# Banded attention with products of 128 rows by 128 columns, keys in two blocks of 128, and the norm ahead of the next mask

## The chip, the cores and the metric

The kernel runs on one core of a Trainium2 chip. The metric is device time in microseconds (us) from one launch, the median of several runs. The engines are named as in the profile: PE (TensorE, matrix products), PEld (its weight loads), DVE (VectorE), ACT (ScalarE), POOL (GpSimd) and SP (SyncE, which issues DMAs here).

## The reference

One inference step of a one-layer encoder: three mixing branches, a gated merge, and a PEER layer of retrieved experts, for a prompt of 512 frames and a sample of 32 frames of a running stream. The change touches one branch, the sliding-window attention. It has 4 KV heads of 4 query heads each, head size 64. A query in chunk c (64 frames) reads the keys of chunks c-2 to c, so 192 keys; a learned sink takes part in the softmax. From `swa_prompt`, where `band` puts the three chunks beside each other:

```python
    kb, vb = band(k), band(v)
    s = jnp.einsum('bnqgrd,bnkgd->bngrqk', q, kb).astype(jnp.float32) * SWA_HEAD_DIM ** -0.5
    koff = jnp.arange(nk) - SWA_BACK_CHUNKS * CHUNK
    s = s + rel_bias(rel_table, koff[None, :] - jnp.arange(CHUNK)[:, None])
...
    s = jnp.where(valid[None, :, None, None, None, :], s, NEG)
    p = sink_softmax(s, sinks).astype(vb.dtype)
    o = jnp.einsum('bngrqk,bnkgd->bnqgrd', p, vb).reshape(B, S, SWA_HEADS * SWA_HEAD_DIM)
```

The sample's 32 queries (`swa_sample`) read a cache of 128 keys and their own 32.

## The kernel before

The program is a row of stages, each between barriers of all engines. In `stage_swa` the order of the work on each engine is written out by hand; semaphore counts (`Steps`) tie the engines together. Beside the attention PE works off a part of the input projection: `later.share` gives it *slices*. A slice is one block of 128 input features of a projection block and takes six products of 128 rows by 128 columns by 272 (L254, L256, L258, two each). Weights for these arrive as pieces of eight slices: SP loads them (L210), POOL splits each in two float32r parts, L221 and L225. `SWA_SHARES = (3, 3, 2, 3, 3, 2)` says how many slices stand at each position of a head; a piece is used up behind each position with two. When a projection block is complete ACT copies it out of PSUM (L420), and the slices of position 6 and position 0 need that buffer again.

The stage first does four projection blocks and loads the bias rows. Then come four heads `g`, each of nine units `u`: chunks 0 to 7 of the prompt, and unit 8, the sample. In a unit 2 pairs of query heads lie side by side as 128 rows. PE's order in a unit is: scores of u+1 (L1492, stationary the queries, 64 rows by 128 columns), two or three slices, transposes of the probabilities `pn` of u (L1510, one for each block of 64 keys and pair), values of u-1 (L1527, stationary 64 rows by 64 columns of `v_tok`). A float32 product counts as two instructions in the profile, a transpose as one. DVE masks the scores (L1643), puts the sink beside them (L1648), takes the maximum (L1651), and norms: reciprocal (L1658) and product `pn` (L1663). ACT takes the exponentials (L1571), copies the transposed probabilities to `p_t` (L1582) and the result out (L1597). Key count is 64 in chunk 0, 128 in chunk 1, 192 from chunk 2 on, 160 in the sample. In the profile `128*64 128x128` is a stationary side of 128 rows and 64 columns and a moving side of 128 columns.

## Time and profile before

| | us |
|---|---|
| median of 3 runs (lowest, highest) | 5074.0 (5071.29, 5079.49) |
| the profiled execution, its span | 5081.78, 5080.0 |
| PE busy in the span | 4933.8 (97%) |
| DVE, ACT, POOL busy | 3172.1, 1100.0, 2855.1 |
| ahead of the heads of `stage_swa` | 1165 to 1224 |
| the four heads of `stage_swa` | 1224 to 1443 |

Busy PE is time in which at least one product is in flight; products are pipelined, so it does not say at what pace they go. Start times in the timeline do. PEclk in a window is the mean granted clock as a share of 2.4 GHz, whose other level is 1.2 GHz.

### The profile page before, as it was taken

What the parts mean: (1) busy time and instruction counts of PE and PEld (TensorE: products, weight loads), DVE (VectorE), ACT (ScalarE), POOL (GpSimd) and SP (SyncE); (2) the same over time, 40 slices, a digit from 0 to 9 for tenths busy, and PEclk for the clock granted to TensorE, in tenths of its full rate; (3) what the DMA queues carried; (4) which work ended last, traced back from release to release, by engine and by line L of the source; (5) the groups of instructions that cost most, each with busy time, mean ns of one, the idle gap of its engine ahead of it and who ended that gap; (6) DMA issues with size and microseconds to landing.
All of it is one profiled execution on the core that took longest, in us unless ns stands there. A gap on an engine that the chain in (4) does not pass through costs nothing. (4 is left out here: it accounts for less than half of the span.)

```text
span 5080.0 us, 87718 instructions
## 1 busy us (share of the span) xinstructions
PE 4933.8 (97%) x32144; PEld 4804.1 (95%) x32144; DVE 3172.1 (62%) x4701; ACT 1100.0 (22%) x1607; POOL 2855.1 (56%) x1698
## 2 busy tenths in 40 slices
PE   8999999999999998999999999999999999999998
PEld 8999999998888787999999999999999999999998
DVE  5477777772222433413057886888786888888865
ACT  4133333331322433201012111122221000000001
POOL 7400000004223333555567787888887999999986
PEclk9999999999999999999999999999999999999999
DMA  7333333334233445533334337889998888888852
GB/s 266 108 127 126 126 126 126 126 127 121 89 110 145 149 165 191 176 131 120 111 131 140 136 131 283 327 323 326 326 328 302 293 311 303 311 301 313 301 201 105
DMA packets 343019, 1010.57 MB, mean 199 GB/s; under 512 B 39696, under 2 KB 132080, under 8 KB 307200
## 3 DMA queue, kind: packets, MB, share of 16 engines
q1 hardware_dynamic: 165760, 526.23, 30.1%
q0 software_dynamic: 36864, 268.45, 14.0%
q10 hardware_dynamic: 140192, 213.34, 11.9%
q8 instruction: 109, 1.79, 0.1%
q14 instruction: 94, 0.77, 0.0%
HBM read 882.26 MB, written 126.76 MB: 199 GB/s over the span
## 5 line engine op out<-in xcount | busy, mean ns | idle before, releaser
L221 POOL TENSOR_SCALAR w_hi<-w_raw 128x1024 fp32r<-128x1024 f32 x702 | 778.7, 1109 | 1983.0 <-PE ps L753 940.1
L225 POOL TENSOR_TENSOR w_lo<-w_raw,w_hi 128x1024 fp32r<-128x1024 f32 x702 | 1734.2, 2470 | 131.8 <-POOL w_hi L221 128.1
L254 PE MATMUL ps<-h_hi,w_hi 128*128 128x416 f32 (+1 forms) x3936 | 1137.1, 328 | 25.5 <-POOL w_lo L225 7.2
L258 PE MATMUL ps<-h_hi,w_lo 128*128 128x416 f32 (+1 forms) x3936 | 1118.5, 323 | 0.0
L256 PE MATMUL ps<-h_lo,w_hi 128*128 128x416 f32 (+1 forms) x3936 | 1111.3, 322 | 0.0
L254 PEld LDWEIGHTS ps<-h_hi,w_hi 128*128 128x128 f32 x3936 | 687.9, 190 | 44.5 <-issue 40.0
L254 PE MATMUL ps<-ex_c_hi,w_hi 128*128 128x416 f32 x2048 | 719.1, 351 | 9.5 <-DVE ex_c_lo L2877 8.6
L258 PE MATMUL ps<-ex_c_hi,w_lo 128*128 128x416 f32 x2048 | 723.9, 353 | 0.0
L256 PE MATMUL ps<-ex_c_lo,w_hi 128*128 128x416 f32 x2048 | 715.9, 350 | 0.0
L256 PEld LDWEIGHTS ps<-h_lo,w_hi 128*128 128x128 f32 x3936 | 687.8, 190 | 6.0
L258 PEld LDWEIGHTS ps<-h_hi,w_lo 128*128 128x128 f32 x3936 | 685.3, 190 | 2.8
L2904 DVE TENSOR_TENSOR ex_y<-ps,ex_y 128x416 f32<-128x416 f32 x512 | 296.9, 585 | 202.4 <-PE ps L258 200.7
L751 PE MATMUL ps<-in_t_hi,w_hi 128*128 128x272 f32 x1408 | 405.4, 288 | 0.9 <-ACT rows_out L866 0.9
L753 PE MATMUL ps<-in_t_hi,w_lo 128*128 128x272 f32 x1408 | 405.7, 288 | 0.0
L752 PE MATMUL ps<-in_t_lo,w_hi 128*128 128x272 f32 x1408 | 405.5, 288 | 0.0
L254 PEld LDWEIGHTS ps<-ex_c_hi,w_hi 128*128 128x128 f32 x2048 | 385.1, 188 | 13.1 <-issue 10.9
L256 PEld LDWEIGHTS ps<-ex_c_lo,w_hi 128*128 128x128 f32 x2048 | 385.7, 188 | 6.4
L258 PEld LDWEIGHTS ps<-ex_c_hi,w_lo 128*128 128x128 f32 x2048 | 384.9, 188 | 2.3
L2291 DVE SCALAR_TENSOR_TENSOR g_sb_u_rows<-g_sb_u_rows,ps 128x2048 f32<-128x2048 f32 x128 | 291.8, 2280 | 139.1 <-DMA g_sb_u_rows<-peer_u,sp_expert 138.9
L730 DVE TENSOR_TENSOR w_lo<-in_sums,w_hi 128x1024 fp32r<-128x1024 f32 x176 | 215.6, 1226 | 206.2 <-ACT w_hi L708 204.1
L2303 DVE SCALAR_TENSOR_TENSOR ps<-ex_v_rows,sp_dot,ps 128x2048 f32<-128x2048 f32 x127 | 297.8, 2345 | 15.5 <-DMA ex_v_rows<-peer_v,sp_expert 15.5
L753 PE MATMUL ps<-h_hi,w_lo 128*128 128x272 f32 x1056 | 304.5, 288 | 0.0
(319 smaller groups left out, 8168.4 us busy)
## 6 DMA issues: line engine op xcount, KB each, us to landing
w_raw<-weights SPq DMA_DIRECT2D x906, 512.0 KB, 3.8
up<-up_out ACTq DMA_DIRECT2D x128, 208.0 KB, 5.7
gate<-g_sb_g ACTq DMA_DIRECT2D x13, 2048.0 KB, 15.0
proj<-rows_out ACTq DMA_DIRECT2D x97, 272.0 KB, 2.0
sp_first<-up ACTq DMA_DIRECT2D x16, 832.0 KB, 7.4
ex_up<-up ACTq DMA_DIRECT2D x16, 832.0 KB, 9.0
ex_gate<-gate ACTq DMA_DIRECT2D x16, 832.0 KB, 17.9
sp_first<-proj ACTq DMA_DIRECT2D x48, 272.0 KB, 3.6
```

Of the source, the lines that this page charges most:

```text
L221: pool.tensor_scalar(self.whi[:, slot, :], self.raw[:, slot, :], 1.0, 1.0, ALU.mult, ALU.mult).then_inc(self.hi_done, 1)
L225: pool.tensor_tensor(self.wlo[:, slot, :], self.raw[:, slot, :], self.whi[:, slot, :].bitcast(F32), ALU.subtract).then_inc(self.split_done, 1)
L254: pe.matmul(acc, hi, x, start=first, stop=False)
L256: pe.matmul(acc, hi, x, start=False, stop=False)
L258: mm = pe.matmul(acc, lo, x, start=False, stop=last)
L730: dve.tensor_tensor(self.core.wlo[:, slot, :], self.source(name), self.core.whi[:, slot, :].bitcast(F32), ALU.subtract).then_inc(self.did_ ...
L751: pe.matmul(out, hi, x_hi(k), start=k == 0, stop=False)
L752: pe.matmul(out, hi, x_lo(k), start=False, stop=False)
L753: mm = pe.matmul(out, lo, x_hi(k), start=False, stop=k == PIECE_K - 1)
L2291: dve.scalar_tensor_tensor(row_of_slot, row_of_slot, 1.0, self.token_rows, ALU.mult, ALU.mult, accum_out=self.dot[:, s:s + 1]).then_inc(se ...
L2303: dve.scalar_tensor_tensor(self.token_rows, buf[:, s % GATHERS, :], c, self.token_rows, ALU.mult, ALU.add).then_inc(self.summed, 1)
L2904: dve.tensor_tensor(y[:, j, 0:TD], ps[:, 4 + j % 4, 0:TD], y[:, j, 0:TD], ALU.add).then_inc(added, 1)
```

## The change

Tiles with 64 rows get 128, the upper half zero (written by DVE at the start of the stage, PE waits for it on `cleared`), so that the scores' products have 128 rows. Keys go in blocks of 128: two transposes a pair in place of three, into 128 rows; `v_tok` holds at each chunk the 128 tokens from its start, so a value product takes 128 rows by 128 columns (the second 64 columns are the next tile's and their results are not read), two blocks in place of three. The last 64 columns of the second block of `pn` are zero for the prompt. On DVE, `normed(u)` stands ahead of `masked(u + 1)`.

```diff
-        q, q_s = two("q", [SWA_HD, N_CHUNKS, SWA_GROUP, CHUNK]), two("q_s", [SWA_HD, SWA_GROUP, DEC_SEQ])
-        k, v = two("k", [SWA_HD, T]), two("v", [SWA_HD, T])
-        cache_k, cache_v = two("cache_k", [SWA_HD, SWA_WINDOW]), two("cache_v", [CHUNK, 2, SWA_HD])
-        v_tok = sb("v_tok", [CHUNK, NB, SWA_HD])
+        q, q_s = two("q", [P, N_CHUNKS, SWA_GROUP, CHUNK]), two("q_s", [P, SWA_GROUP, DEC_SEQ])
+        k, v = two("k", [P, T]), two("v", [SWA_HD, T])
+        cache_k, cache_v = two("cache_k", [P, SWA_WINDOW]), two("cache_v", [SWA_WINDOW, 2, SWA_HD])
+        v_tok = sb("v_tok", [SWA_WINDOW, NB + 1, SWA_HD])
...
-        pn = sb("pn", [P, 2, 2, BAND])
-        p_t = sb("p_t", [CHUNK, 2, 2, 3 * P])
+        pn = sb("pn", [P, 2, 2, 2 * SWA_WINDOW])
+        p_t = sb("p_t", [SWA_WINDOW, 2, 2, 2 * P])
...
-                dve_names += [f"s{u + 1}", f"sink{u + 1}", f"max{u + 1}"]
+                dve_names += [f"inv{u}", f"pn{u}", f"s{u + 1}", f"sink{u + 1}", f"max{u + 1}"]
...
-                return 2 * DEC_SEQ, SWA_WINDOW + DEC_SEQ, [CHUNK, CHUNK, DEC_SEQ]
-            n = min(u, 2) + 1
-            return P, n * CHUNK, [CHUNK] * n
+                return 2 * DEC_SEQ, SWA_WINDOW + DEC_SEQ, [SWA_WINDOW] * 2
+            n_keys = (min(u, 2) + 1) * CHUNK
+            return P, n_keys, [min(n_keys, SWA_WINDOW)] + [SWA_WINDOW] * (n_keys > SWA_WINDOW)
+
+        def span_of(u):
+
+            return (SEQ, DEC_SEQ) if u == N_CHUNKS else (u * CHUNK, min(SWA_WINDOW, SEQ - u * CHUNK))
...
-            sp.dma_start(k[n][:, :], k_rows[g]).then_inc(head_loaded[n], 16)
+            sp.dma_start(k[n][0:SWA_HD, :], k_rows[g]).then_inc(head_loaded[n], 16)
...
-            sp.dma_start(cache_v[n][:, :, :], io["cache_sv"][g].rearrange("(b t) d -> t b d", t=CHUNK)
-                         ).then_inc(head_loaded[n], 16)
+            sp.dma_start(q_s[n][0:SWA_HD, :, :], of_head[:, :, SEQ:T]).then_inc(head_loaded[n], 16)
+            sp.dma_start(cache_k[n][0:SWA_HD, :], io["cache_sk"][g]).then_inc(head_loaded[n], 16)
+            sp.dma_start(cache_v[n][:, 0, :], io["cache_sv"][g]).then_inc(head_loaded[n], 16)
...
             pe.wait_ge(rows_copied, 1)
+            pe.wait_ge(dve_s.sem, dve_s.at("cleared"))
...
-                                          pn[0:n_rows, u % 2, pair, j * CHUNK:j * CHUNK + w],
+                                          pn[0:n_rows, u % 2, pair, j * SWA_WINDOW:j * SWA_WINDOW + w],
...
-                        if u < N_CHUNKS:
-                            values = v_tok[0:w, u + 1 - len(widths) + j, :]
+                        if u == N_CHUNKS and j == 0:
+                            values = cache_v[g % 2]
                         else:
-                            values = cache_v[g % 2][:, j, :] if j < 2 else v_tok[0:w, N_CHUNKS, :]
-                        mm = pe.matmul(ps[0:SWA_HD, 4 + u % 2, pair * n_rows:(pair + 1) * n_rows], values,
+                            tile = max(u - 2, 0) if j == 0 else u
+                            values = v_tok[0:w, tile:tile + 2, :]
+                        mm = pe.matmul(ps[:, 4 + u % 2, pair * n_rows:(pair + 1) * n_rows],
+                                       values.rearrange("t two d -> t (two d)"),
...
-                for b, (t0, w) in enumerate(BLOCKS):
+                for b in units:
+                    t0, w = span_of(b)
...
-                n = len(widths) * n_rows
-                if u < N_CHUNKS:
-                    i = act.activation(p_t[:, u % 2, :, 0:n], ps[0:CHUNK, 2:4, 0:n], ACT.Copy)
-                else:
-                    act.activation(p_t[:, u % 2, :, 0:2 * n_rows],
-                                   ps[0:CHUNK, 2:4, 0:2 * n_rows], ACT.Copy)
-                    i = act.activation(p_t[0:DEC_SEQ, u % 2, :, 2 * n_rows:n],
-                                       ps[0:DEC_SEQ, 2:4, 2 * n_rows:n], ACT.Copy)
+                i = act.activation(p_t[0:w, u % 2, :, 0:n], ps[0:w, 2:4, 0:n], ACT.Copy)
...
+                full = N_CHUNKS - 1
+                act.activation(v_tok[:, 0:full, :],
+                               ps[:, 4, 0:full * SWA_HD].rearrange("t (b d) -> t b d", d=SWA_HD), ACT.Copy)
+                act.activation(v_tok[0:CHUNK, full, :], ps[0:CHUNK, 4, full * SWA_HD:N_CHUNKS * SWA_HD],
+                               ACT.Copy).then_inc(*act_s.did("v0"))
...
+            for n in range(2):
+                for x in (q[n], q_s[n], k[n], cache_k[n]):
+                    dve.memset(x[SWA_HD:P], 0.0)
+                dve.memset(cache_v[n][:, 1, :], 0.0)
+            dve.memset(v_tok[:, N_CHUNKS - 1:NB + 1, :], 0.0)
+            dve.memset(pn[:, :, :, :], 0.0).then_inc(*dve_s.did("cleared"))
...
                 for u in units:
+                    normed(u, g)
                     if u + 1 < NB:
                         masked(u + 1, g)
-                    normed(u, g)
```

The other tiles are sliced `[0:SWA_HD]` where DMAs write them, as `k` is here.

PE, head 0 of the stage, one full chunk (`ps` is PSUM, `x5` stands for five such rows, the last two rows begin the next slices), before:

```order
L1510 MATMUL ps<-const_sb,swa_sb_pn 64x128 [waits swa_dve,swa_act]
L1510 MATMUL ps<-const_sb,swa_sb_pn 64x128 x5
L1527 MATMUL ps<-swa_sb_p_t,swa_sb_v_tok 64x128 [waits swa_act]
L1527 MATMUL ps<-swa_sb_p_t,swa_sb_v_tok 64x128 x5
L1492 MATMUL ps<-swa_sb_k,swa_sb_q 128x192 [waits swa_dve]
L1492 MATMUL ps<-swa_sb_k,swa_sb_q 128x192
L254 MATMUL ps<-h_hi,w_hi 128x272 [waits split_done]
L254 MATMUL ps<-h_hi,w_hi 128x272
```

and in the changed kernel (its L1513, L1531 and L1495 are L1510, L1527 and L1492 of before):

```order
L1513 MATMUL ps<-const_sb,swa_sb_pn 128x128 [waits swa_dve,swa_act]
L1513 MATMUL ps<-const_sb,swa_sb_pn 128x128 x3
L1531 MATMUL ps<-swa_sb_p_t,swa_sb_v_tok 128x128 [waits swa_act]
L1531 MATMUL ps<-swa_sb_p_t,swa_sb_v_tok 128x128 x3
L1495 MATMUL ps<-swa_sb_k,swa_sb_q 128x192 [waits swa_dve]
L1495 MATMUL ps<-swa_sb_k,swa_sb_q 128x192
L254 MATMUL ps<-h_hi,w_hi 128x272 [waits split_done]
L254 MATMUL ps<-h_hi,w_hi 128x272
```

Transposes go from six to four, value products from six to four, all of 128 result rows; the order and the semaphores waited for stay.

DVE, from the start of head 0, before:

```order
L1643 SCALAR_TENSOR_TENSOR swa_sb_s<-ps,swa_sb_bias 128x2x64 [waits swa_bias_loaded,swa_table_loaded,swa_pe]
L1648 COPY swa_sb_s<-swa_sb_sinks 128x2
L1651 TENSOR_REDUCE swa_sb_neg_max<-swa_sb_s 128x2 [waits swa_dve]
L1643 SCALAR_TENSOR_TENSOR swa_sb_s<-ps,swa_sb_bias 128x2x128 [waits swa_pe]
L1648 COPY swa_sb_s<-swa_sb_sinks 128x2
L1651 TENSOR_REDUCE swa_sb_neg_max<-swa_sb_s 128x2 [waits swa_dve]
L1658 RECIPROCAL swa_sb_inv<-swa_sb_total 128x2 [waits swa_act]
L1663 TENSOR_TENSOR swa_sb_pn<-swa_sb_p,swa_sb_inv 128x2x64 [waits swa_dve]
```

and in the changed kernel (L1651, L1656, L1659, L1666, L1671 are L1643, L1648, L1651, L1658, L1663 of before), behind the memsets:

```order
L1651 SCALAR_TENSOR_TENSOR swa_sb_s<-ps,swa_sb_bias 128x2x64 [waits swa_bias_loaded,swa_table_loaded,swa_pe]
L1656 COPY swa_sb_s<-swa_sb_sinks 128x2
L1659 TENSOR_REDUCE swa_sb_neg_max<-swa_sb_s 128x2 [waits swa_dve]
L1666 RECIPROCAL swa_sb_inv<-swa_sb_total 128x2 [waits swa_act]
L1671 TENSOR_TENSOR swa_sb_pn<-swa_sb_p,swa_sb_inv 128x2x64 [waits swa_dve]
L1651 SCALAR_TENSOR_TENSOR swa_sb_s<-ps,swa_sb_bias 128x2x128 [waits swa_pe]
L1656 COPY swa_sb_s<-swa_sb_sinks 128x2
L1659 TENSOR_REDUCE swa_sb_neg_max<-swa_sb_s 128x2 [waits swa_dve]
```

The reciprocal and `pn` of chunk 0 moved from behind the mask and maximum of chunk 1 to ahead of them, and so on through the head.

## Rows read from the trace of the kernel before

**Rows 1.** The page: busy time, share of the span and count of instructions of each engine.

```profile
PE 4933.8 (97%) x32144; PEld 4804.1 (95%) x32144; DVE 3172.1 (62%) x4701; ACT 1100.0 (22%) x1607; POOL 2855.1 (56%) x1698
```

**Rows 2.** Windows ahead of the heads, heads 0, 2, 3: us, busy PE PEld DVE ACT POOL, PEclk.

```profile
1165.00:1224.30 59.30, 54.77 (x405) 53.45 (x403) 0.00 (x0) 2.87 (x5) 24.30 (x15) 0.94 0.70 170
1224.30:1279.00 54.70, 51.16 (x372) 44.45 (x372) 18.57 (x45) 21.22 (x60) 18.12 (x12) 0.97 0.17 54
...
1334.00:1388.50 54.50, 52.13 (x392) 45.47 (x390) 15.64 (x45) 19.94 (x59) 14.85 (x9) 1.00 0.34 107
1388.50:1443.00 54.50, 50.57 (x368) 43.90 (x367) 16.69 (x45) 19.96 (x59) 10.97 (x7) 0.97 0.08 25
```

**Rows 3.** Waits of PE, 1224 to 1443 us: total us, times, longest.

```profile
PE ps L1510 <- DVE swa_sb_pn L1663: 10.0, 14, 2.0
PE ps L1510 <- ACT swa_sb_p L1571: 1.5, 1, 1.5
```

**Rows 4.** Timeline, one chunk of head 3: start us, us, engine, line, operation.

```profile
1405.41 0.42 PE L258 MATMUL ps<-h_hi,w_lo 128*128 128x272 f32 x2
...
1405.66 0.82 PE L1510 MATMUL ps<-const_sb,swa_sb_pn 128*64 128x128 f32 x6
...
1408.52 0.56 DVE L1643 SCALAR_TENSOR_TENSOR swa_sb_s<-ps,swa_sb_bias 128x384 f32<-128x384 f32 x1 [4.11 <-PE ps L1492]
...
1409.77 0.15 DVE L1658 RECIPROCAL swa_sb_inv<-swa_sb_total 128x2 f32<-128x2 f32 x1
1409.99 0.46 ACT L1571 ACTIVATE swa_sb_p<-swa_sb_s,swa_sb_neg_max 128x193 f32<-128x193 f32 x1 [2.00 <-DVE swa_sb_inv L1658]
1410.10 0.56 DVE L1663 TENSOR_TENSOR swa_sb_pn<-swa_sb_p,swa_sb_inv 128x384 f32<-128x384 f32 x1 [0.18 <-DVE swa_sb_inv L1658]
...
1410.79 0.19 ACT L1571 ACTIVATION_READ_ACCUMULATOR swa_sb_p<-swa_sb_s,swa_sb_neg_max 128x1 f32 x1
1410.80 0.81 PE L1510 MATMUL ps<-const_sb,swa_sb_pn 128*64 128x128 f32 x6 [0.76 <-DVE swa_sb_pn L1663]
...
1411.55 1.52 PE L1527 MATMUL ps<-swa_sb_p_t,swa_sb_v_tok 64*64 64x128 f32 x12
...
1411.75 2.34 POOL L225 TENSOR_TENSOR w_lo<-w_raw,w_hi 128x1024 fp32r<-128x1024 f32 x1 [0.18 <-POOL w_hi L221]
...
1413.00 0.91 PE L1492 MATMUL ps<-swa_sb_k,swa_sb_q 64*128 64x192 f32 x4
...
1414.20 0.41 PE L256 MATMUL ps<-h_lo,w_hi 128*128 128x272 f32 x2
...
1416.38 0.82 PE L1510 MATMUL ps<-const_sb,swa_sb_pn 128*64 128x128 f32 x6
```

**Rows 5.** Groups by form on PE, 1223 to 1444 us: count, busy us, mean ns.

```profile
L1527 PE MATMUL ps<-swa_sb_p_t,swa_sb_v_tok 64*64 64x128 f32 x336 | 43.4, 274 | 0.0
L1510 PE MATMUL ps<-const_sb,swa_sb_pn 128*64 128x128 f32 x168 | 23.9, 275 | 11.6 <-DVE swa_sb_pn L1663 10.0 <-ACT swa_sb_p L1571 1.5
```

**Rows 6.** Timeline of PE in the memory stage, products of 128 rows by 128 columns.

```profile
1519.24 1.16 PE L1785 MATMUL ps<-ma_sb_p_t,ma_sb_v_tok 128*128 128x128 f32 x8
1520.15 0.49 PE L254 MATMUL ps<-h_hi,w_hi 128*128 128x272 f32 x2
...
1527.96 1.03 PE L1761 MATMUL ps<-ma_sb_k,ma_sb_q 128*128 128x256 f32 x4
...
1529.08 0.41 PE L256 MATMUL ps<-h_lo,w_hi 128*128 128x272 f32 x2
```

**Rows 7.** Timeline, head 3, chunk 2: VectorE beside GpSimd.

```profile
1395.92 2.40 POOL L225 TENSOR_TENSOR w_lo<-w_raw,w_hi 128x1024 fp32r<-128x1024 f32 x1 [0.18 <-POOL w_hi L221]
...
1396.52 1.82 DVE L1648 COPY swa_sb_s<-swa_sb_sinks 128x2 f32<-128x2 f32 x1
...
1399.83 0.38 PE L1510 MATMUL ps<-const_sb,swa_sb_pn 128*64 128x128 f32 x2 [1.53 <-ACT swa_sb_p L1571]
```

**Rows 8.** Window behind the wait in rows 7; the columns as in rows 2.

```profile
1400.00:1405.00 5.00, 5.00 (x25) 4.20 (x24) 1.81 (x5) 2.12 (x8) 0.00 (x0) 0.66 0.00 0
```

More of the change, by code:

```diff
@@ L1401, in stage_swa @@
                 act_names += [f"e{u + 1}_0", f"e{u + 1}_1"]
-                dve_names += [f"s{u + 1}", f"sink{u + 1}", f"max{u + 1}"]
+                dve_names += [f"inv{u}", f"pn{u}", f"s{u + 1}", f"sink{u + 1}", f"max{u + 1}"]
             pe_names += [f"t{u}"] + ([f"o{u - 1}"] if u else [])
             act_names += [f"t{u}"] + ([f"o{u - 1}"] if u else [])
-            dve_names += [f"inv{u}", f"pn{u}"]
         pe_s = Steps(sem("pe"), pe_names + [f"o{NB - 1}"])
         act_s = Steps(sem("act"), act_names + [f"o{NB - 1}"])
-        dve_s = Steps(sem("dve"), dve_names)
+        dve_s = Steps(sem("dve"), dve_names + [f"inv{NB - 1}", f"pn{NB - 1}"], ["cleared"])
         def geometry(u):
             if u == N_CHUNKS:
-                return 2 * DEC_SEQ, SWA_WINDOW + DEC_SEQ, [CHUNK, CHUNK, DEC_SEQ]
-            n = min(u, 2) + 1
-            return P, n * CHUNK, [CHUNK] * n
+                return 2 * DEC_SEQ, SWA_WINDOW + DEC_SEQ, [SWA_WINDOW] * 2
[3 more added lines that the diff above has]
+            return (SEQ, DEC_SEQ) if u == N_CHUNKS else (u * CHUNK, min(SWA_WINDOW, SEQ - u * CHUNK))
         beside = lambda g: LATER_START + LATER_SWA * g if isinstance(g, int) else LATER_SWA * g + LATER_START
@@ L1432, in load @@
             for r in range(SWA_GROUP):
-                sp.dma_start(q[n][:, :, r, :], of_head[:, r, 0:SEQ].rearrange("d (c t) -> d c t", t=CHUNK)
+                sp.dma_start(q[n][0:SWA_HD, :, r, :], of_head[:, r, 0:SEQ].rearrange("d (c t) -> d c t", t=CHUNK)
                              ).then_inc(head_loaded[n], 16)
-            sp.dma_start(q_s[n][:, :, :], of_head[:, :, SEQ:T]).then_inc(head_loaded[n], 16)
-            sp.dma_start(cache_k[n][:, :], io["cache_sk"][g]).then_inc(head_loaded[n], 16)
-            sp.dma_start(cache_v[n][:, :, :], io["cache_sv"][g].rearrange("(b t) d -> t b d", t=CHUNK)
-                         ).then_inc(head_loaded[n], 16)
+            sp.dma_start(q_s[n][0:SWA_HD, :, :], of_head[:, :, SEQ:T]).then_inc(head_loaded[n], 16)
+            sp.dma_start(cache_k[n][0:SWA_HD, :], io["cache_sk"][g]).then_inc(head_loaded[n], 16)
+            sp.dma_start(cache_v[n][:, 0, :], io["cache_sv"][g]).then_inc(head_loaded[n], 16)
         @block.sync
@@ L1576, in copy_transposed @@
                 n_rows, _, widths = geometry(u)
+                w, n = widths[0], len(widths) * n_rows
                 act.wait_ge(pe_s.sem, pe_s.at(f"t{u}", g))
                 held(act)
-                n = len(widths) * n_rows
-                if u < N_CHUNKS:
-                    i = act.activation(p_t[:, u % 2, :, 0:n], ps[0:CHUNK, 2:4, 0:n], ACT.Copy)
-                else:
-                    act.activation(p_t[:, u % 2, :, 0:2 * n_rows],
-                                   ps[0:CHUNK, 2:4, 0:2 * n_rows], ACT.Copy)
-                    i = act.activation(p_t[0:DEC_SEQ, u % 2, :, 2 * n_rows:n],
-                                       ps[0:DEC_SEQ, 2:4, 2 * n_rows:n], ACT.Copy)
+                i = act.activation(p_t[0:w, u % 2, :, 0:n], ps[0:w, 2:4, 0:n], ACT.Copy)
                 i.then_inc(*act_s.did(f"t{u}"))
@@ L1602, in head @@
                 act.wait_ge(pe_s.sem, pe_s.at("v0", g))
-                act.activation(v_tok[:, 0:N_CHUNKS, :],
-                                         ps[0:CHUNK, 4, :].rearrange("t (b d) -> t b d", d=SWA_HD), ACT.Copy).then_inc(*act_s.did("v0"))
+                full = N_CHUNKS - 1
[3 more added lines that the diff above has]
+                               ACT.Copy).then_inc(*act_s.did("v0"))
                 act.wait_ge(pe_s.sem, pe_s.at("v1", g))
```

## Prediction

> **What bounds the kernel now.** I read the page first. PE is busy for 97% of the span [rows 1], so the question in every stage is what PE does in it. The change touches only the sliding-window stage, and there only what lies behind the first projection blocks, so I cut that part into windows, one per KV head: about 54.5 us each, PE busy for 50.6 to 52.1 us of it [rows 2]. A busy PE says little about why, so the next view is that of PE's waits: 10.0 us behind the normalised probabilities `pn` and 1.5 us behind the exponentials, all at the transposes L1510 [rows 3]. The timeline shows the period. From one chunk's first transpose to the next takes 1416.38 - 1410.80 = 5.58 us [rows 4]. PE's own work in it is 1414.20 - 1410.80 = 3.40 us of attention products (with the first two projection products) and sixteen more projection products. A pair of these takes 1405.66 - 1405.41 = 0.25 us, so 2.0 us, 5.40 us in all: even in a chunk with three slices PE waits 0.18 us, and in one with two slices 0.76 us and more. The loop that sets 5.58 us is: scores of chunk u+1 on PE, masking and then norming on DVE, transposes of u on PE, values of u-1, scores of u+2.
>
> **What the change does, part by part.**
>
> *Fewer products.* A full chunk (2 to 7) had 6 transposes, 12 instructions of value products and 4 of scores. It gets 4, 8 and 4. The paces come from the memory stage, whose products are 128 rows by 128 columns already [rows 6]: eight of 128 columns from 1519.24 to 1520.15, 0.114 us each; four of 256 columns and two projection products from 1527.96 to 1529.08, so (1.12 - 0.25)/4 = 0.22 us, hence 0.163 us for 192 columns. At these paces the old chunk would take 18 x 0.114 + 4 x 0.163 + 0.25 = 2.95 us. It takes 3.40 us. The missing 0.45 us lies where the shape changes (128 rows to 64 and back, four times a chunk); in the memory stage nothing is missing. The new chunk is 128 rows throughout: 12 x 0.114 + 0.65 + 0.25 = 2.27 us. That is 1.13 us less, and 27.1 us for the 24 full chunks of four heads. Outside these, of 168 and 336 instructions [rows 5] 112 and 224 remain; 144 of the 168 removed are counted, so 24 x 0.114 = 2.7 us more. I put the shape changes at the head's start, in chunks 0 and 1 and in the decode chunk at three chunks' worth a head, 1.35 us; half stays, since `v`, the first chunk's probabilities and the decode probabilities still have 64 rows: 2.7 us for four heads. Sum of this part: 32.5 us.
>
> *A rule that sizes the same edit.* The row at 1405.66 starts 0.25 us behind the pair before it, so going from 128*128 to 128*64 costs nothing [rows 4]. The Trainium skill (TensorEngine Tiling (Array Packing), Key Properties) says that changing the tiling mode, column tilings among them, drains the engine. By that rule the 36 entries into L1510 would have a drain as well, a quarter of 0.45 us each, and 32.5 us would become about 36 us. The row decides, so I stay with 32.5.
>
> *The norm ahead of the next mask.* It removes the listed waits, 11.5 us [rows 3], and the unlisted 0.18 us of about 16 three-slice chunks, 2.9 us: 14.4 us. What comes in its place is a chain that DVE and ACT now walk strictly in turn for each chunk: mask and maximum 1409.99 - 1408.52 = 1.47 us, the exponentials 1410.98 - 1409.99 = 0.99 us, hand-over 0.14 us, reciprocal and norm 1410.66 - 1409.77 = 0.89 us, 3.49 us in all [rows 4]. PE needs 2.02 us and two or three slices of 0.75 us, 3.52 or 4.27 us a chunk, so PE stays the slower one by a little. `pn` of a chunk is ready 3.7 us behind its scores (0.25 us hand-over); PE asks for it after two sets of slices, 0.46, 0.91 and 0.65 us, at least 5.0 us. So the cover is 1.3 us.
>
> *The clock.* Twice PE stood for 1.5 to 2.0 us, and behind one such wait the window of 5 us has a granted clock of 0.66 [rows 7, 8]: 5 x 0.34 x 2 = 3.4 us at 1.2 GHz, which costs 1.7 us. The first and last head show it (0.97), the third none (1.00) [rows 2]. With those waits gone 3.4 us come back.
>
> *What is late next.* GpSimd's L225 holds something that DVE's small copy L1648 needs: the copy begins at 1396.52 and ends with L225 at 1398.3, 1.82 us long [rows 7]. In the chunk of rows 4 L225 starts at 1411.75, 1.9 us behind the last projection product. That chunk's DVE work lay outside it. In the changed kernel no wait and fewer products stand between those slices and the next scores: 0.46 + 0.91 + 0.65 + 0.25 us puts the mask at 2.3 us and its copy at 2.7 us, inside L225, which ends near 4.2 us. DVE's chain then runs up to 1.5 us late, four times a head. PE has one place without cover: the slices of position 6 need the PSUM buffer that ACT's L420 copies out behind the exponentials of chunk 4. Those end 0.25 + 1.47 + 0.99 = 2.71 us behind the scores, the copy at 3.45 us; PE asks at 1.5 + 2.02 = 3.52 us. Lateness left there falls on PE, and a three-slice chunk makes up only 0.78 us. I take 1.25 us a head, 5 us, from bounds of 0 and 2.4 us (one L225) a head. The first head has the activation table still to load and a row of L225 behind each other; 2 us more, bounds 0 and 4. Sum of new waits: 7 us, between 0 and 14.
>
> *Hidden edits.* DVE's twelve memsets write some 7,000 elements a partition; at 0.56 us for 384 elements [rows 4] that is at most 10 us, once. PE waits for them only behind the first projection blocks, and in the 59 us of these DVE does nothing [rows 2]; without that cover up to 10 us would fall on PE. The second copy of `v_tok` lies beside three slices. The transposed copy on ACT gets shorter (512 elements a row, from 768). DMAs keep count and bytes.
>
> **Sum.** 32.5 + 14.4 + 3.4 - 7 = 43.3 us. The profiled execution took 5081.8 us for a span of 5080.0; it becomes 5038.5. The runs have a median of 5074.0 us, 7.8 lower, so 5031 us, 0.9% less. The stages behind start on a barrier with their own loads and move up as a whole.
>
> **Rivals.**
> *The chain DVE-ACT-GpSimd becomes the bound.* `pn` reads two SBUF tensors. No `pn` in the old trace lies inside an L225, so no row says what happens then. If it too stands until L225 ends, the chain is late by up to 2.4 us at each of 16 pieces, 1.3 us of it covered: 1.1 x 16 = 18 us, with some returns of the low clock 20 us, in place of 7. Time: 5043 us. For it: the copy of rows 7. Against: the cover. The Trainium skill (SBUF — State Buffer, Who interferes with whom) says just this, that a tensor_tensor with both inputs in SBUF contends with GpSimd's reads and the second to issue waits in full; L1648 agrees with it for the copy.
> *Shape changes stay.* If the 0.45 us comes from the kind of product (plain float32 beside the other), padding keeps it: 24 x 0.45 + 2.7 = 13.5 us less, 5044 us. Against it: rows 6, where the same two kinds meet.
> *No gain.* The norm's order gives nothing, since DVE's wait for the exponentials delays the next mask as much as the norm did, and loads of 128 columns for the values are not hidden: then a full chunk stays near its 5.4 us and only the clock and the short waits come back, 24 x 0.18 + 3.4 = 7.7 us: 5066 us. Against: the chain's 3.49 us, and eight products of 128 columns at 0.114 us each with loads as wide [rows 6].
> *Slower.* Each of the 16 L225 falls wholly on PE (2.4 us), and each such wait brings a stretch at 1.2 GHz (1.7 us): 16 x 4.1 = 66 us against 50.3 us of gains, 5090 us. It decides from 12 such waits on, three a head. For it: both parts were seen once each in rows 7 and 8. Against: the cover of 1.3 us and DVE's pace.
>
> **How the numbers follow.** The forecast, 5022 to 5038 us, has 0.62; the chain as bound 0.20 (5038 to 5052); shape changes that stay 0.08 (5040 to 5050); no gain 0.05; slower 0.05, of which half past the bound. 0.2% is 10 us, about what a measurement of this kernel can tell from no change. The forecast and most of the chain's cases lie between 5018 and 5047, which leaves out 2 in 10. Faster 0.93, same 0.04, slower 0.03.
>
> **What the new profile would show.** PE windows of a head of 42 to 44 us with a clock of 1.00; transposes L1513 x112 and values L1531 x224 of the full forms; no idle of PEld between the attention groups; no wait of L1513 for `pn` in the heads 1 to 3, or a short one; the mask's copy L1656 long where it meets L225; a wait of a projection product for L420 once a head. Wrong would be: a period of a full chunk above 4.4 us, value products slower than 0.12 us, waits of PE above 14 us, or heads with a clock below 0.95.

## The result, and the profile after

The changed kernel takes 5038.9 us in the median of four runs (5033.9 to 5042.97), the kernel before 5072.65 us beside it. The ratio is 0.9929, with a 95% interval of 0.9918 to 0.9941: 0.7% faster, where I had said 5031 us and 0.9%. The profiled execution took 5041.12 us for a span of 5039.3, 40.7 us less than the profiled one of before.

Windows of the changed kernel ahead of the heads, of the four heads, and of 7 us in head 0. The columns are those of [rows 2].

```profile
1160.00:1219.20 59.20, 53.49 (x404) 52.22 (x404) 6.46 (x12) 2.87 (x5) 24.62 (x15) 0.97 0.67 171
1219.20:1268.40 49.20, 45.97 (x338) 43.83 (x337) 22.77 (x45) 18.23 (x60) 20.81 (x13) 0.93 0.25 75
1268.40:1313.10 44.70, 42.71 (x338) 41.02 (x337) 20.06 (x45) 17.30 (x59) 13.73 (x9) 1.00 0.30 93
1313.10:1358.30 45.20, 42.85 (x339) 41.07 (x338) 20.15 (x45) 17.29 (x59) 13.73 (x9) 1.00 0.39 125
1358.30:1400.20 41.90, 40.15 (x320) 38.71 (x319) 19.95 (x45) 17.02 (x58) 10.66 (x7) 1.00 0.11 31
1231.00:1238.00 7.00, 6.86 (x27) 6.34 (x28) 3.52 (x10) 2.51 (x10) 0.00 (x0) 0.51 0.00 0
```

From the first transpose of `v` to the last value product, the heads took 1442.32 - 1224.27 = 218.05 us before and 1400.22 - 1219.22 = 181.0 us now. That is 37.05 us. The heads begin 5.05 us earlier than before. Of this 2.7 us come from ahead of the stage, where nothing was changed (its first load is issued at 1161.75 us for 1164.46). Most of the rest is a wait of PE ahead of the heads, 1.2 us for 1.9, and the stretch of 3.4 us at half clock that stood behind it at 1220.6 in the kernel before and is missing here. The kernel with the order alone, whose work ahead of the heads is that of before, lacks the stretch too (its wait is 1.4 us), so this is not a gain of the change that a run shows. Behind the heads 1.4 us are lost. Three heads run at full clock; head 0 does not. DVE's twelve memsets are 6.46 us of the first window, beside PE's projection blocks.

PE's waits in the heads (total us, times, longest), and the two large groups by form, which answer to [rows 3] and [rows 5]:

```profile
PE ps L254 <- POOL w_lo L225: 4.7, 3, 1.6
PE ps L1513 <- DVE swa_sb_pn L1671: 3.9, 5, 3.0
```

```profile
L1531 PE MATMUL ps<-swa_sb_p_t,swa_sb_v_tok 128*128 128x128 f32 x208 | 28.2, 277 | 0.0
...
L1513 PE MATMUL ps<-const_sb,swa_sb_pn 128*128 128x128 f32 x104 | 16.5, 278 | 3.9 <-DVE swa_sb_pn L1671 3.9
```

The waits for `pn` went from 10.0 to 3.9 us, 3.0 of them in one place. Three new ones stand in front of projection products. This view counts a wait only from the modelled end of the product before it, some 0.3 us behind the moment at which PE could have begun. By start times, what a transpose group begins later than the usual 0.13 us behind the last projection product adds up to about 15.7 us before and 5.4 us now. The timeline of PE in one full chunk of head 2:

```profile
1335.70 0.60 PE L1513 MATMUL ps<-const_sb,swa_sb_pn 128*128 128x128 f32 x4
...
1336.14 1.06 PE L1531 MATMUL ps<-swa_sb_p_t,swa_sb_v_tok 128*128 128x128 f32 x8
...
1337.03 0.82 PE L1495 MATMUL ps<-swa_sb_k,swa_sb_q 128*128 128x192 f32 x4
...
1337.55 0.55 PE L254 MATMUL ps<-h_hi,w_hi 128*128 128x272 f32 x2
...
1339.95 0.60 PE L1513 MATMUL ps<-const_sb,swa_sb_pn 128*128 128x128 f32 x4
```

Read the starts, not the durations. Transposes take 0.44 us, values 0.89, scores 0.52, where the old chunk of [rows 4] took 0.75 and 1.45 us for the first two and 0.84 for the scores (its two projection products followed at 1413.84). The period with three slices is 1339.95 - 1335.70 = 4.25 us; I had said 4.27.

Next, one of the three new waits, with what DVE, ACT and POOL do ahead of it:

```profile
1329.66 1.05 POOL L221 TENSOR_SCALAR w_hi<-w_raw 128x1024 fp32r<-128x1024 f32 x1 [4.01 <-PE ps L258]
1329.87 0.86 DVE L1656 COPY swa_sb_s<-swa_sb_sinks 128x2 f32<-128x2 f32 x1
...
1332.38 0.19 ACT L1577 ACTIVATION_READ_ACCUMULATOR swa_sb_p<-swa_sb_s,swa_sb_neg_max 128x1 f32 x1
1332.47 0.60 ACT L420 ACTIVATE later_beside<-ps 128x544 f32<-128x544 f32 x1
...
1333.36 0.49 PE L254 MATMUL ps<-h_hi,w_hi 128*128 128x272 f32 x2 [1.56 <-POOL w_lo L225]
```

The profile names L225. PE starts 0.29 us behind the end of ACT's L420 (1332.47 + 0.60 = 1333.07), and 0.30 us behind it in the two other places (copies at 1287.30 and 1377.03, products at 1288.20 and 1377.93). That is the place the prediction named, "the slices of position 6". The naming is checked by an experiment below.

Finally head 0, DVE's chain ahead of the 3.0 us wait:

```profile
1225.01 2.18 DVE L1656 COPY swa_sb_s<-swa_sb_sinks 128x2 f32<-128x2 f32 x1
1227.33 0.42 DVE L1659 TENSOR_REDUCE swa_sb_neg_max<-swa_sb_s 128x2 f32<-128x258 f32 x1
1228.90 0.17 DVE L1666 RECIPROCAL swa_sb_inv<-swa_sb_total 128x2 f32<-128x2 f32 x1 [1.14 <-ACT swa_sb_p L1577]
1229.21 1.78 DVE L1671 TENSOR_TENSOR swa_sb_pn<-swa_sb_p,swa_sb_inv 128x256 f32<-128x256 f32 x1
```

```profile
1224.80 2.37 POOL L225 TENSOR_TENSOR w_lo<-w_raw,w_hi 128x1024 fp32r<-128x1024 f32 x1 [0.18 <-POOL w_hi L221]
...
1228.37 2.34 POOL L225 TENSOR_TENSOR w_lo<-w_raw,w_hi 128x1024 fp32r<-128x1024 f32 x1 [0.18 <-POOL w_hi L221]
```

The copy of two elements ends at 1227.19 with the first L225 (1227.17), and the norm of the same chunk ends at 1230.99, 0.28 us behind the second (1230.71). PE stands from 1228.2 to 1231.14 and then runs at half clock for 6.8 us.

### The profile page after: what moved, and what is told of

It reads as the page before. It is cut to its first block and busy times, and to the rows that moved or that the text cites. A ratio compares the mean times of both kernels' runs of the same rounds, so it can differ in the third digit from the quotient of the medians.

```text
span 5039.3 us, 87347 instructions
## 1 busy us (share of the span) xinstructions
PE 4899.0 (97%) x31952; PEld 4785.1 (95%) x31952; DVE 3191.5 (63%) x4713; ACT 1089.4 (22%) x1607; POOL 2858.5 (57%) x1698
## 5 line engine op out<-in xcount | busy, mean ns | idle before, releaser
L221 POOL TENSOR_SCALAR w_hi<-w_raw 128x1024 fp32r<-128x1024 f32 x702 | 777.8, 1108 | 1942.1 <-PE ps L753 940.1
L225 POOL TENSOR_TENSOR w_lo<-w_raw,w_hi 128x1024 fp32r<-128x1024 f32 x702 | 1736.3, 2473 | 131.8 <-POOL w_hi L221 128.1
## 6 DMA issues: line engine op xcount, KB each, us to landing
gate<-g_sb_g ACTq DMA_DIRECT2D x13, 2048.0 KB, 14.4
```

Source lines behind the costliest of these rows:

```text
L221: pool.tensor_scalar(self.whi[:, slot, :], self.raw[:, slot, :], 1.0, 1.0, ALU.mult, ALU.mult).then_inc(self.hi_done, 1)
L225: pool.tensor_tensor(self.wlo[:, slot, :], self.raw[:, slot, :], self.whi[:, slot, :].bitcast(F32), ALU.subtract).then_inc(self.split_done, 1)
```

## The experiments

My theory: the gain is two independent parts, products (about 32 us) and norm order (about 14 us), less the new wait behind L420 and the trouble of head 0. Rivals: the order gives nothing or depends on the products; 128 rows and columns don't matter; L225 itself is what PE waits for; the heads are paced by DVE and ACT, not by PE. Heads are given below as the sum over all four, from the one traced execution of each kernel, since medians of one kernel scatter by some 4 us. Where no wait stands in them these sums repeat well: heads 1 to 3 of three kernels below (the moved copy, both edits, head 0) agree within 0.15 us each. Head 0 does not repeat so well, since its clock may fall or not. The ratio is always to the kernel before.

**The order alone** (kernel before, only this changed, with the semaphore names to match):

```diff
                 for u in units:
+                    normed(u, g)
                     if u + 1 < NB:
                         masked(u + 1, g)
-                    normed(u, g)
```

> The kernel before, with its 64-row and 64-column products, and only VectorE's order changed: the reciprocal and norm of chunk u stand ahead of the mask of chunk u+1. My theory (two separate gains: about 14 us from the order, 27 to 32 us from the products): PE then walks its own work without the 10 us of waits for pn, heads of about 50 us in place of 54.5, heads together 200 to 204 us (218 before), time 14 to 17 us less than before, near 5057 us. Rival (the order gives nothing, since VectorE's wait for the exponentials now delays the next mask): heads stay at 53 to 55 us, time within 5 us of before. Second rival (the loop was bound by something both parts need): the order alone gives more than 20 us.

Measured: 5060.5 us, ratio 0.9971 (0.996 to 0.9981), 12.8 us less than the kernel before beside it, for 14 to 17 expected. Heads 203.6 us, 14.4 us less than before. Of these 1.7 are the clock (one stretch of 3.4 us at half clock in the heads, for two before). Heads 1 and 2 of this kernel:

```profile
1275.40:1325.80 50.40, 50.40 (x386) 45.02 (x385) 20.82 (x45) 19.29 (x59) 14.13 (x9) 1.00 0.26 83
1325.80:1376.20 50.40, 50.40 (x386) 45.00 (x385) 18.03 (x45) 19.41 (x59) 14.52 (x9) 1.00 0.35 112
```

PE is busy for 50.40 of 50.40 us. With the new order PE no longer waits in heads 1 to 3, and what is left there is its own work. Head 0 keeps one wait for `pn`, of 2.6 us. By start times the waits in front of the transposes went from 15.7 to 2.8 us. The two rivals fall.

**The products alone** (changed kernel, DVE's loop in the old order):

```diff
                 for u in units:
-                    normed(u, g)
                     if u + 1 < NB:
                         masked(u + 1, g)
+                    normed(u, g)
```

> The changed kernel with VectorE's old order (mask of u+1 ahead of the norm of u); 128-row products and two blocks of 128 keys stay. Theory: PE's own work in a full chunk is 1.13 us shorter, but the loop through VectorE and ScalarE (scores, mask, norm, transposes, values) is no longer hidden, so PE waits for pn in nearly every chunk; the parts do not add: 20 to 28 us less than before, 5045 to 5053 us, waits of L1513 for pn of 20 us or more. Rival (the products give their full 32 us whatever the order): within 12 us of the changed kernel's 5039 us, waits for pn near 15 us. Rival (the products give nothing alone): within 5 us of before.

Measured: 5053.3 us, ratio 0.9957 (0.994 to 0.9973), heads 195.4 us, 22.6 us less than before. PE's waits in its heads:

```profile
PE ps L1514 <- DVE swa_sb_pn L1672: 19.1, 27, 2.8
```

The shorter products made PE arrive earlier at a `pn` that was no earlier: 10.0 us of waits became 19.1 (by start times 15.7 became 26.5). Part of the product gain is spent there. Yet the two parts alone, 14.4 and 22.6 us, add up to 37.0, just what both together give. That is no proof that they are free of each other: with the low clock taken out they are 12.7 and 20.9, 33.6 us for 37.05, and on either side another wait swallows a part of what the products save, the one for `pn` here, the one behind L420 and that of head 0 in the changed kernel. The full 31 us show only where both are gone, in the kernel under "Head 0".

**Scores on 64 rows** (changed kernel):

```diff
-   q[g % 2][:, u, 2 * pair:2 * pair + 2, :].rearrange("d h t -> d (h t)"),
-   k[g % 2][:, t0 + CHUNK - n_keys:t0 + CHUNK], start=True, stop=True)
+   q[g % 2][0:SWA_HD, u, 2 * pair:2 * pair + 2, :].rearrange("d h t -> d (h t)"),
+   k[g % 2][0:SWA_HD, t0 + CHUNK - n_keys:t0 + CHUNK], start=True, stop=True)
```

(`q_s` and `cache_k` likewise.)

> The changed kernel with the scores' products on 64 rows again (queries, keys and cached keys cut to the 64 rows that hold data); all else stays, and no result changes. This undoes only the padding of the scores. Theory (going from 128 rows to 64 and back costs PE time at every score group): about 0.4 us for each of 36 score groups, 14 us, of which a part may hide where PE waits anyway: 9 to 14 us slower than the changed kernel. Rival (the 0.45 us of the old chunk came from the kind of product, and the rows do not matter): within 3 us of the changed kernel.

**Values 64 columns wide** (changed kernel):

```diff
-                            values = v_tok[0:w, tile:tile + 2, :]
-                        mm = pe.matmul(ps[:, 4 + u % 2, ...],
+                            values = v_tok[0:w, tile, :]
+                        mm = pe.matmul(ps[0:SWA_HD, 4 + u % 2, ...],
```

(`cache_v` likewise.)

> The changed kernel with the value products 64 columns wide (one tile of v_tok as the stationary side, results in 64 PSUM rows), on 128 rows. Moving columns are the same, 128 a product. Theory from the row of before in which 128 by 64 transposes followed 128 by 128 products without a gap: nothing, within 3 us of the changed kernel, or a little faster for half as many weight columns. Rival (the Trainium skill, TensorEngine Tiling (Array Packing), Key Properties: a change of tiling mode drains the engine, column tilings included): two entries and exits at each of 36 value groups, about 0.2 to 0.3 us a group, 7 to 11 us slower.

Measured: 5040.9 us and 5038.7 us, ratios 0.9929 (0.9912 to 0.9945) and 0.993 (0.9913 to 0.9946). By the time alone "no difference" would have won in both (the rival for the rows, the theory for the columns): the heads are 182.2 and 183.0 us for 181.0. The timelines say otherwise. First the scores on 64 rows, then the values of 64 columns, the same chunk of head 2 as above:

```profile
1338.26 0.60 PE L1513 MATMUL ps<-const_sb,swa_sb_pn 128*128 128x128 f32 x4
1338.70 1.06 PE L1531 MATMUL ps<-swa_sb_p_t,swa_sb_v_tok 128*128 128x128 f32 x8
1339.68 0.92 PE L1495 MATMUL ps<-swa_sb_k,swa_sb_q 64*128 64x192 f32 x4
1340.53 0.52 PE L254 MATMUL ps<-h_hi,w_hi 128*128 128x272 f32 x2
```

```profile
1336.48 0.60 PE L1513 MATMUL ps<-const_sb,swa_sb_pn 128*128 128x128 f32 x4
1337.01 1.09 PE L1531 MATMUL ps<-swa_sb_p_t,swa_sb_v_tok 128*64 128x128 f32 x8
1338.03 0.92 PE L1495 MATMUL ps<-swa_sb_k,swa_sb_q 128*128 128x192 f32 x4
1338.64 0.55 PE L254 MATMUL ps<-h_hi,w_hi 128*128 128x272 f32 x2
```

With 64 rows the values-to-scores step is 0.98 us for 0.89 and the scores-to-slices step 0.85 for 0.52: 0.42 us more in these rows, 0.39 in the mean step once the slices behind, 0.03 shorter, are counted. With 64 columns the three steps are 0.53 for 0.44, 1.02 for 0.89 and 0.61 for 0.52: 0.31 us more. Both shapes do cost PE time in each chunk. Head 2 gives it back at one place: the step from the scores to the slices of position 6, 2.38 us in the changed kernel, is 0.97 us with 64 rows and 1.45 us with 64 columns. PE came later to a wait whose end did not move.

**ScalarE's copy ahead of the exponentials** (changed kernel):

```diff
-                    if u + 1 < NB:
-                        exps(u + 1, g)
                     if (u + 3) % len(SWA_SHARES) == 0:
                         later.scalar(act, beside(g) + (u + 3) // len(SWA_SHARES) - 1)
+                    if u + 1 < NB:
+                        exps(u + 1, g)
```

> The changed kernel with one move on ScalarE: where a head copies a finished projection block out of PSUM (L420, position 6), the copy stands ahead of the exponentials of the next chunk in place of behind them. Theory (the waits at the slices of position 6 that the profile puts down to GpSimd's L225 are in truth for this copy, since PE starts 0.29 us behind its end each time): the three waits of 1.55 to 1.58 us in heads 0 to 2 go, 3.5 to 5 us less than the changed kernel, while the exponentials of that chunk come 0.6 us later and stay covered. Rival (the waits are for GpSimd's split weights, as the profile names it): no change, within 1 us, and the same three waits.

Measured: 5031.1 us, ratio 0.9919 (0.9905 to 0.9932); heads 175.1 us, 5.9 us less than the changed kernel's. Its head 1, which has none of PE's long waits left:

```profile
1270.10:1312.90 42.80, 42.54 (x339) 41.08 (x338) 19.79 (x45) 16.82 (x59) 13.78 (x9) 1.00 0.32 98
```

The three waits that the profile had put down to L225 are gone, and L225 was not touched. In head 2 these slices now run while an L225 does:

```profile
1330.15 2.38 POOL L225 TENSOR_TENSOR w_lo<-w_raw,w_hi 128x1024 fp32r<-128x1024 f32 x1 [0.18 <-POOL w_hi L221]
...
1330.77 0.54 PE L254 MATMUL ps<-h_hi,w_hi 128*128 128x272 f32 x2
```

The wait was for L420; it is shown, not only argued. The gain is above the 3.5 to 5 us expected, because the price had been read from the view of waits (1.55 us each). By start times the step from the scores to these slices was 2.37 to 2.39 us for a usual 0.52, so 1.86 us each.

**Fewer copies of the sinks** (changed kernel; `SINK_AT = (0, 1, N_CHUNKS)`):

```diff
-                dve.tensor_copy(s[0:n_rows, u % 2, :, 0:1], ...)
+                if u in SINK_AT:
+                    dve.tensor_copy(s[0:n_rows, u % 2, :, 0:1], ...)
```

> The changed kernel with VectorE's copy of the sinks beside the scores (L1656) only in units 0, 1 and 8: the other chunks find the sinks still there from the last use of that half of the tile. Seven of nine copies a head go minus one, 24 of 36 in all. Theory (VectorE's chain is held where a copy lands inside GpSimd's L221 or L225, and part of this reaches PE at position 6 and in head 0): the removed copies give 0.1 us each on a covered chain and 0.7 us at each of three position-6 waits: 1 to 4 us less. Rival (all of it is covered): within 1 us. Rival (pn then meets L225 instead of the copy, and stands just as long): 0 to 1 us, with more long rows of L1671.

Measured: 5033.9 us, ratio 0.9923 (0.9909 to 0.9936); heads 173.6 us. Heads 1 and 3 are as short as with the other edit (42.7 and 40.1), head 2 is 44.1 with a wait for L420 left. Of the 7.4 us less, 3.4 are the clock: head 0 had no low stretch here, though its 3.0 us wait was the same. That leaves 4.0 us, the upper end of the forecast. Norms of over 0.9 us number ten for eight in the changed kernel, as the last rival had it, but they did not use up the gain. (The expectation says 24 of 36 copies go; that is right, and the words "minus one" in it are not: six of nine a head.)

**Both edits:** the two diffs above together.

> Both edits together: the projection copy ahead of the exponentials, and the sink copies only in units 0, 1 and 8. Theory (they remove the same wait from two sides): 4 to 6 us less than the changed kernel, hardly more than the first edit alone. Rival (each has its own wait): the sum of the two.

Measured: 5035.8 us, ratio 0.9923 (0.9909 to 0.9936), heads 174.8 us, 42.7, 42.7 and 40.1 for heads 1 to 3 and 49.3 for head 0. In the heads the two remove one wait from two sides, as the theory had it: 6.2 us less than the changed kernel, where the sum of the two would be 9.9 without the clock. The median is 3.1 us lower than the changed kernel's and no lower than that of either edit alone, so the times rank nothing here; the heads do.

**Both narrow shapes again, without the wait** (each on top of the moved copy):

> The kernel with ScalarE's projection copy moved ahead of the exponentials (the edit of e4_acc_early), and the scores' products on 64 rows again. In e3_rows64 alone the 64 rows cost PE 0.39 us a full chunk by the start times (value products to scores 0.987 for 0.893 us, scores to projection 0.844 for 0.518), yet the heads kept their length; in head 2 each such excess was given back at the wait in front of the slices of position 6, 1.4 us shorter. Theory (the padding is a real gain of PE that the wait for ScalarE's copy swallows): without that wait the heads grow to 44.5 us from 42.8 in e4_acc_early, all four together 182 to 184 us from 175.1, 7 to 9 us slower than e4_acc_early. Rival (the head is paced by VectorE and ScalarE in any case, not by PE): heads together 175 to 177 us.

> The same base (e4_acc_early) with value products of 128 rows by 64 columns. In e6_cols64 PE took 0.32 us more a full chunk by its start times (transposes to values 0.529 for 0.436 us, values to scores 1.018 for 0.893, scores to projection 0.620 for 0.518), and the heads kept their length as well. Theory (as for the rows: real, and swallowed by one wait): heads 1 to 3 about 1.3 us longer each than in e4_acc_early, together 5 to 6 us more, 180 to 181 us. Rival (paced by VectorE and ScalarE): within 2 us of e4_acc_early's 175.1.

Measured: 5037.6 us, ratio 0.9928 (0.9915 to 0.9942), and 5043.3 us, ratio 0.9938 (0.9925 to 0.9952). Head 1 of each, 64 rows first:

```profile
1264.80:1309.50 44.70, 44.50 (x339) 41.32 (x338) 18.98 (x45) 17.28 (x59) 14.34 (x9) 1.00 0.30 93
```

```profile
1269.20:1313.80 44.60, 43.87 (x339) 40.41 (x338) 20.39 (x45) 17.00 (x59) 13.73 (x9) 1.00 0.31 93
```

Heads 1 to 3 together take 131.4 and 130.8 us where the base takes 125.7: 1.9 and 1.7 us a head, all at full clock. So the shapes matter as soon as PE is what a head waits for, and "paced by VectorE and ScalarE" falls. My sum for four heads with 64 rows (182 to 184 us) missed the measured 178.2, because head 0 happened to have no low stretch (3.4 us) and a wait of 1.8 us in place of 3.0; I had not allowed for either.

**Head 0** (on top of both edits, with the copy left in unit 8 alone, `SINK_AT = (N_CHUNKS,)`):

```diff
+            act.activation(p[0:1, 0, 0, 0:1], ident[0:1, 0:1], ACT.Exp)
             later.scalar(act, 0)
...
+            def sinks_ahead(g):
+                for half in range(2):
+                    i = dve.tensor_copy(s[:, half, :, 0:1], pairs_at(sinks[:, :], 2, 4 * g).unsqueeze(2))
+                i.then_inc(*dve_s.did("sink0"))
...
+                sinks_ahead(g)
                 masked(0, g)
```

> The kernel of e7_both with two edits for the first head: ScalarE takes one exponential of a single element at the start of the stage, so that its table load of 1.28 us lies there, and VectorE copies the sinks of a head into both halves of the score tile ahead of the head's first scores. Theory (head 0 is 49.2 us in place of 42.8 because its second norm comes 3.0 us late, through the table load, a copy held 2.0 us by GpSimd's L225 and a norm held 1.2 us, and the low clock that follows costs 3.4 us more): the 3.0 us wait falls under 1 us, the stretch of low clock at 1231 does not come, head 0 takes 43 to 45 us, and all heads 168 to 171 us (174.8 in e7_both), 4 to 6 us less. Rival (the wait moves to another place of head 0, since POOL's row of L225 stays): head 0 above 46 us.

Measured: 5024.7 us, ratio 0.9905 (0.989 to 0.992), heads 168.3 us:

```profile
1217.60:1260.30 42.70, 42.48 (x338) 41.05 (x337) 20.26 (x39) 16.87 (x59) 21.07 (x13) 1.00 0.26 83
1260.30:1303.10 42.80, 42.56 (x339) 41.09 (x338) 19.95 (x39) 16.98 (x59) 13.78 (x9) 1.00 0.32 97
1303.10:1345.80 42.70, 42.32 (x338) 41.01 (x338) 18.33 (x39) 17.09 (x59) 14.05 (x9) 1.00 0.41 132
1345.80:1385.90 40.10, 39.92 (x320) 38.74 (x319) 17.95 (x37) 16.81 (x58) 10.72 (x7) 1.00 0.12 32
```

```profile
PE ps L1514 <- DVE swa_sb_pn L1679: 0.4, 2, 0.2
```

Head 0 is now as short as the others and the 3.0 us wait is 0.2. By start times the transposes still begin 1.4 us late in all, and the first slices behind each of heads 0 to 2 still stand for L420, so this is close to PE's own work but not all of it. By time it is below the changed kernel as well, though the two intervals of the ratio just touch (0.992 and 0.9918); the heads, 12.7 us shorter (3.4 of them clock), are clear. Which of its two edits does how much was not tried apart.

**The norm with one tensor input** (on top of that):

```diff
-                dve.tensor_tensor(
-                    pn[...], p[0:n_rows, u % 2, :, 1:1 + n_keys],
-                    inv[0:n_rows, u % 2, :].unsqueeze(2).to_broadcast([n_rows, 2, n_keys]), ALU.mult)
+                for pair in range(2):
+                    i = dve.tensor_scalar(pn[...], p[0:n_rows, u % 2, pair, 1:1 + n_keys],
+                                          inv[0:n_rows, u % 2, pair:pair + 1], None, ALU.mult)
```

> The kernel of e10_head0 with the norm written as two tensor_scalar instructions (one for each pair, the reciprocal as the scalar operand) in place of one tensor_tensor with two SBUF inputs. Question: is it the two inputs that let GpSimd's L225 hold the norm? Theory: a tensor_scalar of 192 elements from SBUF to SBUF is held in the same way, since the two-element copy with one input was held too; long rows of the norm (1.0 us and more) stay, about as many as in e10_head0 (five or more in four heads). Rival: with one tensor input it runs beside L225, rows of 0.3 us and none above 0.5. Either way the heads are paced by PE and their sum stays at 168 to 170 us; time within 5 us of e10_head0.

Measured: 5026.4 us, ratio 0.9901 (0.9884 to 0.9917), heads 169.3 us. The norm's instructions of the base, and of this kernel (duration in ns: shortest, median, longest):

```profile
L1679 DVE TENSOR_TENSOR swa_sb_pn<-swa_sb_p,swa_sb_inv x36: 292/560/2757, 1221.2 to 1380.8; 128x384 f32<-128x384 f32 x24, 128x128 f32<-128x128 f32 x4, 128x256 f32<-128x256 f32 x4, 64x320 f32<-64x320 f32 x4
```

```profile
L1680 DVE TENSOR_SCALAR swa_sb_pn<-swa_sb_p,swa_sb_inv x72: 245/314/2457, 1222.1 to 1382.9; 128x192 f32<-128x192 f32 x48, 128x64 f32<-128x64 f32 x8, 128x128 f32<-128x128 f32 x8, 64x160 f32<-64x160 f32 x8
```

Instructions above 0.9 us number 12 in the base and 13 here. A norm with one tensor input stands as well, so the second input is not needed for it; the rival falls. What makes each form stand, these runs do not say. And a norm that stands for up to 2.8 us costs PE little in either kernel: the transposes begin 1.4 and 2.5 us late in all of the heads, by start times.

## Why the prediction was right, and where its numbers were off

By its mechanism the forecast case came true: PE stays the bound, both parts pay, and the new waits lie where they were put. By the time alone this could not be said. 5038.9 us lies 0.9 us above the range given to the forecast case (5022 to 5038) and inside that of "the chain as bound" (5038 to 5052); it is the windows and the waits that tell the two apart. Term by term, for the heads in the trace (low clock taken out at half its length, 3.4 us of 6.8 us in both kernels):

| term | predicted | measured | from |
|---|---|---|---|
| norm order | 14.4 | 15.45 | 218.05 - 3.4 to 3 x 50.4 + 48.0 = 199.2, heads of the first experiment with head 0 taken as long as heads 1 and 2 |
| products | 32.5 | 30.9 | that 199.2 to the 168.3 of the head-0 kernel |
| clock | 3.4 | 0 | 6.8 us at 1.2 GHz before and after |
| new waits | -7 | -9.3 | 181.0 - 168.3 less the clock's 3.4 |
| sum in the heads | 43.3 | 37.05 | 37.05 seen directly |

*Products.* By the start times a full chunk lost 0.31 us at the transposes (0.75 to 0.44), 0.56 at the values and 0.33 at the scores, and 0.04 came back in the slices: 1.16 us, for 1.13 predicted. Both halves of it hold as well. Within a group the single starts are 109 to 112 ns apart in either kernel, so two transposes and four instructions of values fewer are 0.67 us (0.68 predicted), and 0.49 us remain for the shapes (0.45 predicted). The 0.39 and 0.31 us of the two narrow variants add up to more than 0.49 because each makes the step between values and scores anew. What is missing from 32.5 to 30.9 lies outside the full chunks (24 x 1.16 = 27.8 us in them, so 3.1 us outside for 5.4 predicted).

*The row that decided against the rule.* From "The row at 1405.66 starts 0.25 us behind the pair before it" I concluded that columns of 64 cost nothing. For that transpose it holds. For the value products it fails: 0.31 us a chunk. The Trainium skill (TensorEngine Tiling (Array Packing), Key Properties) says that a change of tiling mode drains the engine; by the single starts, the first product of a group follows the last one of the group before after 109 to 112 ns where the shape stays and 202 to 205 ns where it changes, in rows (scores on 64) or in columns (values of 64) alike. The second start of such a group is late as well, 160 ns behind the first for 111 (values) and 267 for 165 (scores). By the rule I had made 36 us of the product part, by counting the entries into L1510 too; measured are 30.9. The rule fits the products, and the row was right for transposes of 64 columns.

*Norm order.* The measured 15.45 takes head 0 as if it had no wait; it agrees with the 15.7 us of late transposes that the start times of before show. The chain was predicted at 3.49 us and takes 3.51 (mask at 1338.03 to the end of `pn` at 1341.54). PE's 4.25 us period with three slices is longer, and the waits for `pn` in heads 1 to 3 are below 1 us in all.

*Clock.* "With those waits gone 3.4 us come back" is the step that failed. The 2.0 us waits of before went, but a new one of 3.0 us in head 0 brought 6.8 us at half clock, as much as before. I had the wait ("2 us more" for the first head) and did not carry it on to the clock.

*New waits.* 5 + 2 us became 9.3: 6.2 in heads 1 to 3, of which 5.6 at position 6 (1.86 us each by start times, 1.56 in the view of waits) and the rest where norms come late, and 3.1 in head 0 beside its clock. At the ends of heads 0 to 2 the slices stand for L420 too, but there the step from the last value product to the slices is 0.48 us in the head-0 kernel as well, so it is no part of the 9.3. The place was right, the price 1.86 us for 1.25. (My expectation of the moved copy calls the three heads 0 to 2; they are 1 to 3. In head 0 the step at position 6 is 0.78 us for 0.52, at full clock.)

*The chain as a rival.* Its mechanism is true and its price is not. Eight `pn` in the heads take 1.8 to 2.7 us for a usual 0.42 to 0.56. Each begins inside an L225 and ends 0.27 to 0.42 us behind its end, so they stand until it ends, as the Trainium skill (SBUF — State Buffer, Who interferes with whom) has it for the port pair that the two engines share. But the cover of a chunk takes nearly all of it, and it is larger than the 1.3 us of the prediction. That figure counted two sets of two slices in a row between the scores and the transposes, which `SWA_SHARES` never has. In the kernel with the shortest heads the norm of chunk 7 stands 2.2 us longer than usual (2.76 us for 0.56) and the transposes behind it begin 0.05 us late, so the cover is about 2.1 us there. That kernel has twelve such rows, 0.4 us of listed waits for `pn` and 1.4 us by start times. "Shape changes stay", "no gain" and "slower" fall by the windows above.

*The total.* The trace gave 40.7 us where I had 43.3. That it came so near is in part luck: the heads gave 37.05, and the other 3.6 us lie ahead of and behind them, where I had put nothing and where no run ties them to the change. The rest of the miss, from 5031 to 5038.9, is how I went from one execution to the median. I carried over that the profiled execution of before was 7.8 us above its median. The one of after was 2.2 us above its own. An offset of one execution is chance, and the difference of medians is 33.8 us, with the traces 6.9 us further apart.

## What to carry to other kernels

When a change makes the engine that is the bound shorter, look for the first place where it meets a hand-over that does not move (here a PSUM buffer copied out behind another engine's longer work): until that is moved, single parts of the change measure as worth nothing, though each costs or saves its time in the start times. Price a shape by start-to-start times of the product groups themselves, and not by the pace of another shape or of a transpose. And put the small work of the other engine (a copy of two elements, a table load) where nobody waits for its chain.

## What the runs showed of the hardware that was not expected

- A group of float32 products whose shape differs from the one before, by 64 rows or by 64 columns, starts 202 to 205 ns behind its last product and not 109 to 112, and its second start is 50 ns (values) to 100 ns (scores) late as well. So the first gap alone understates the price. The step from the last score product to the projection's first is 28 ns from 128 rows and 253 ns from 64, the dearest of them. Transposes of 64 columns between groups of 128 by 128 show no such step (129 ns behind the projection, 109 ns to the scores behind them). Transposes on 64 rows do: they begin 216 ns behind the projection. Why the one kind is exempt stays open.
- GpSimd's L221, a tensor_scalar, holds DVE's copy as well as L225 does: the copy at 1329.87 takes 0.86 us for a usual 0.16 and ends with L221 (1330.73 beside 1330.71). The norm as tensor_scalar with one tensor input is held too, up to 2.46 us. DVE's mask (its input in PSUM) and its maximum next to them keep their 0.56 us.
- A wait of PE in head 0 of 2.9 to 3.0 us was followed by 6.8 us at 1.2 GHz in the changed kernel and in four of its variants (values of 64 columns with and without the moved copy, the moved copy, both edits), and by none in the variant with fewer copies. A wait of 2.6 us brought 6.8 us (scores on 64 rows) or 3.4 us (order alone), one of 2.8 us 3.4 us (products alone), one of 1.8 us nothing. What decides this stays open; for sums it means that a wait of this length can cost 3.4 us more, half of that, or nothing.
- A wait named by the profile for one of two semaphores can be for the other. The test is the constant distance: 0.29 us from the end of L420 each time.
